# The first norm's modulations computed with the weight tiles as stationary operand

## The reference, cut to what matters

```
mod   = silu(c)     @ w_mod + b_mod      # w_mod is 1024 x 6144
mod_c = silu(c_ctx) @ w_mod + b_mod
sh1, sc1, ... = split(mod, 6);  sh1c, sc1c, ... = split(mod_c, 6)
hc = rmsnorm(ctx, norm1_g) * (1 + sc1c) + sh1c
hx = rmsnorm(x,   norm1_g) * (1 + sc1)  + sh1
proj_x = hx @ w_in                       # then four mixers, gates, FFN, second block
```

## Time and profile before

| | |
|---|---|
| median of 3 runs | 1709.49 us (1703.62 to 1711.7) |
| profiled execution | 1702.95 us |
| its span in the profile | 1701.1 us |
| PE busy | 1641.2 us, 96% of the span |
| PEld busy | 1333.6 us, 78% |
| DVE busy | 909.9 us, 53% |
| ACT busy | 625.5 us, 37% |
| mean granted TensorE clock | 0.984 |

### The profile page before, as it was taken

The page is one execution under the profiler, slowest core; times in us unless marked ns, Lnnn a source line. Parts: engine busy times, 40 slices in busy tenths (PEclk is TensorE's granted clock), DMA queues, the critical chain, the costliest instruction groups (busy, mean ns, idle before and its releaser), DMA issues.

```text
span 1701.1 us, 20100 instructions
## 1 busy us (share of the span) xinstructions
PE 1641.2 (96%) x7909; PEld 1333.6 (78%) x7909; DVE 909.9 (53%) x1248; ACT 625.5 (37%) x805; POOL 92.6 (5%) x130
## 2 busy tenths in 40 slices
PE   8999999899999899999999999999999999999997
PEld 3578778678887688888888889977767788888885
DVE  5774686477666544544344565235776544444323
ACT  2342467422223333333333433245754322222221
POOL 0100000111110000000000100003330000000000
PEclk9999999999999899999999999999999999999998
DMA  9332001544553233332333421223442243332331
GB/s 321 126 119 89 29 25 44 181 163 161 196 173 124 62 105 92 92 97 84 100 87 107 124 75 52 75 64 89 101 126 75 79 113 97 91 93 69 101 102 49
DMA packets 227363, 176.68 MB, mean 104 GB/s; under 512 B 15812, under 2 KB 213316, under 8 KB 227270
## 3 DMA queue, kind: packets, MB, share of 16 engines
q1 hardware_dynamic: 220662, 151.23, 30.5%
q0 software_dynamic: 6608, 24.19, 4.3%
HBM read 166.84 MB, written 2.13 MB: 99 GB/s over the span
## 4 chain that ended last, share of the span: by engine, by line
PE 82%; DVE 10%; ACT 5%; issue 2%; DMA 1%; DVEq 0%; POOL 0%; SPq 0%; POOLq 0%; ACTq 0%
PE PS L452 23%; PE PS L454 23%; PE PS L453 23%; PE PS L2300 2%; DVE T L92 1%; DVE WL L92 1%; PE PS L461 1%; PE PS L586 1%; ACT WH L88 1%; PE PS L976 1%; ACT NTP L88 1%; PE PS L473 1%; PE PS L475 1%; PE PS L474 1%; DMA MSRC<-in_w_mod 1%
## 5 line engine op out<-in xcount | busy, mean ns | idle before, releaser
L452 PE MATMUL PS<-XH,WH 128*128 128x512 f32 (+1 forms) x1280 | 489.6, 382 | 12.5 <-DVE WL L92 10.6
L453 PE MATMUL PS<-XL,WH 128*128 128x512 f32 (+1 forms) x1280 | 484.6, 379 | 0.0
L454 PE MATMUL PS<-XH,WL 128*128 128x512 f32 (+1 forms) x1280 | 484.3, 378 | 0.0
L92 DVE TENSOR_TENSOR WL<-WS,WH 128x2048 fp32r<-128x2048 f32 (+1 forms) x129 | 272.5, 2112 | 214.1 <-ACT WH L88 211.6
L452 PEld LDWEIGHTS PS<-XH,WH 128*128 128x128 f32 x1280 | 239.9, 187 | 61.4 <-DVE WL L92 13.6
L454 PEld LDWEIGHTS PS<-XH,WL 128*128 128x128 f32 x1280 | 239.8, 187 | 45.7
L453 PEld LDWEIGHTS PS<-XL,WH 128*128 128x128 f32 x1280 | 240.0, 188 | 44.4 <-issue 0.7
L88 ACT ACTIVATE WH<-WS 128x2048 fp32r<-128x2048 f32 (+1 forms) x129 | 228.6, 1772 | 71.1 <-PE PS L454 46.7
L452 PE MATMUL PS<-HH,WH 128*128 128x512 f32 x352 | 137.2, 390 | 0.2 <-DVE WL L92 0.2
L453 PE MATMUL PS<-HL,WH 128*128 128x512 f32 x352 | 136.9, 389 | 0.0
L454 PE MATMUL PS<-HH,WL 128*128 128x512 f32 x352 | 136.9, 389 | 0.0
(11 more groups left out here) (359 smaller groups left out, 2245.6 us busy)
## 6 DMA issues: line engine op xcount, KB each, us to landing
WS<-in_w_in SPq DMA_DIRECT2D x24, 1024.0 KB, 5.4
WS<-in_ffn_w_up SPq DMA_DIRECT2D x44, 512.0 KB, 5.0
WS<-in_ffn_w_in SPq DMA_DIRECT2D x44, 512.0 KB, 5.0
MSRC<-in_w_mod POOLq DMA_DIRECT2D x32, 512.0 KB, 4.9
WS<-in_fox_w_in SPq DMA_DIRECT2D x16, 1024.0 KB, 5.6
WS<-in_ffn_w_down SPq DMA_DIRECT2D x16, 704.0 KB, 4.5
WS<-in_ffn_w_out SPq DMA_DIRECT2D x16, 704.0 KB, 4.5
MODW<-in_w_mod SPq DMA_DIRECT2D x8, 1024.0 KB, 10.9
```

The source lines that it names most:

```text
L92: self.e.tensor_tensor(o, a, b, op).then_inc(*self.done.to(*key))
L452: e.matmul(o, lh, rh, start=first and i == 0, stop=False)
L453: e.matmul(o, lh, rl, start=False, stop=False)
L454: ins = e.matmul(o, ll, rh, start=False, stop=last and i == n - 1)
```

## The change

`mod_pe(i)` swaps the two operands. The stationary operand is now a 128x128 piece of the tile, and the two columns of `CA` move through it: 2 halves x 8 rows, 16 instructions a tile instead of 8. The result is already a column for each 128 channels, so `MROW`, `mod_turn_pe`, `mod_rows_dve` and `mod_dve` go. Tiles are paired, i with i + 4: tile p holds shifts and tile p + 4 the scales of the norm's rows 2p and 2p + 1. `mods_dve(p)` adds the bias and makes the scale of these two rows as soon as tile p + 4 is done. The four pairs use banks 7, 5, 0 and 1.

The order changes on every engine. PE: filt1, tile 0, filt2, tile 4, filt3 0 to 2, the sums, tile 1, filt3 3 and 4, the spread, tile 5, filt3 5 to 7, spectrum 0, tile 2, spectrum 1, tiles 6, 3 and 7, spectrum 2 and 3. SP loads `x` right after tile 0, and the tiles in the order 0, 4, 1, 5, 2, 6, 3, 7, with `dft` ahead of the last four. ACT squares three rows before the second sine and copies the spread from the bank to `RST`. DVE multiplies each row of the norm once, by scale and inverse together (`norm1_scaled_dve`); ACT adds the shift in its rounding and DVE in the low half. Spectrum 0 and 1 wait for `mods` 1 and 0, because their banks are shared.

```diff
@@ -181,7 +181,6 @@
-    MROW = zone("MROW", [2, 2048], F32, 36)
     KR = zone("KR", [128, 4, L], F32, 0)
@@ -198,7 +197,7 @@
     MODW = [sbt(f"MODW{i}", [128, 8, 256], F32, o) for i, o in enumerate(
-        (WO[0], WO[1], WO[0] + 8 * U8, WO[1] + 8 * U8, FIX + 16 * U8, FIX, FIX + 8 * U8, XO))]
+        (WO[0], WO[1], WO[0] + 8 * U8, WO[1] + 8 * U8, FIX + 16 * U8, FIX, FIX + 8 * U8, ZO + 24 * U8))]
@@ -577,34 +576,36 @@
+    MPAIR = (7, 5, 0, 1)
...
+        p = i % 4
         e.wait_ge(*landed(f"mod_in{i}"))
...
             e.wait_ge(*acts.at("cact"))
-        for k in range(8):
-            ins = e.matmul(bank(4 + i // 2, 256, p1=2, off=256 * (i % 2)), CA[:, :, k], MODW[i][:, k, :],
-                           start=k == 0, stop=k == 7)
+        if i in (2, 3):
+            e.wait_ge(*dve.at("filt", 7))
+        for m in range(2):
+            for k in range(8):
+                ins = e.matmul(bank(MPAIR[p], 2, off=4 * (i // 4) + 2 * m), MODW[i][:, k, 128 * m:128 * m + 128],
+                               CA[:, :, k], start=k == 0, stop=k == 7)
         ins.then_inc(*pe.to("w", i))
-    def mod_turn_pe(e, b):
-        if b == 0:
-            e.wait_ge(*landed("ident"))
-        e.wait_ge(*dve.at("mod_rows", b))
-        for m in range(4 * b, 4 * b + 4):
-            ins = e.matmul(bank(4, 2, off=256 + 2 * m), MROW[:, 128 * m:128 * m + 128], ID[0:2, 0:2], start=True, stop=True)
-        ins.then_inc(*pe.to("mod_turned", b))
-    def mod_rows_dve(v, b):
-        v.e.wait_ge(*pe.at("w", 2 * b + 1))
-        v.cp(MROW[:, 512 * b:512 * b + 512], bank(4 + b, p1=2), key=("mod_rows", b))
-    def mod_dve(v):
-        v.e.wait_ge(*pe.at("mod_turned", 3))
-        c = VOFF["b_mod"]
-        v.tt(MT[:, 0:16, :], bank(4, 32, off=256).rearrange("p (m j) -> p m j", j=2),
-             VT[:, c:c + 16].unsqueeze(2).broadcast_to([128, 16, 2]), ALU.add, key=("mods",))
+    def mods_dve(v, p):
+        v.e.wait_ge(*pe.at("w", 4 + p))
+        c, g1 = VOFF["b_mod"], VOFF["norm1_g"]
+        v.tt(MODT[:, 0:32].rearrange("p (h q) -> p h q", h=2)[:, :, 4 * p:4 * p + 4].rearrange(
+                 "p h (m j) -> p h m j", j=2),
+             bank(MPAIR[p], 8).rearrange("p (h m j) -> p h m j", h=2, j=2),
+             VT[:, c:c + 16].rearrange("p (h q) -> p h q", h=2)[:, :, 2 * p:2 * p + 2].unsqueeze(3).broadcast_to(
+                 [128, 2, 2, 2]), ALU.add, key=("mods", p))
+        a = SM[:, A1 + 2 * p:A1 + 2 * p + 2]
+        v.ts(a, MT[:, 8 + 2 * p:10 + 2 * p, 0], 1.0, None, ALU.add)
+        v.tt(a, a, VT[:, g1 + 2 * p:g1 + 2 * p + 2], ALU.mult)
@@ -633,12 +634,12 @@
             e.wait_ge(*pool.at("row0"))
-        if i == 2:
-            e.wait_ge(*dve.at("mods"))
+        if i < 2:
+            e.wait_ge(*dve.at("mods", 1 - i))
         if i >= 2:
...
         if i == 3:
-            e.wait_ge(*dve.at("norm1", "rooted", 7))
+            e.wait_ge(*acts.at("norm1", "inverse"))
         for odd in range(2):
@@ -662,29 +663,30 @@
         mod_pe(e, 0)
-        mod_pe(e, 1)
         e.wait_ge(*landed("filt_w2"))
...
         e.matmul(bank(1, p1=64), FW2[:, :], FS1[0:64, :], start=True, stop=True).then_inc(*pe.to("filt2"))
-        mod_pe(e, 2)
-        mod_pe(e, 3)
-        mod_turn_pe(e, 0)
         mod_pe(e, 4)
-        e.wait_ge(*pool.at("ones"))
+        for n in range(3):
+            filt3_pe(e, n)
         e.wait_ge(*dve.at("norm1", "sum", 7))
         sums_pe(e, "norm1", T[2], L, True, True, ("norm1", "sums"), step=1)
+        mod_pe(e, 1)
+        filt3_pe(e, 3)
+        filt3_pe(e, 4)
+        e.wait_ge(*landed("ident"))
+        spread_pe(e, "norm1", L)
         mod_pe(e, 5)
-        mod_turn_pe(e, 1)
-        spread_pe(e, "norm1", L)
+        for n in range(5, 8):
+            filt3_pe(e, n)
+        spectrum_pe(e, 0)
+        mod_pe(e, 2)
+        spectrum_pe(e, 1)
         mod_pe(e, 6)
-        mod_turn_pe(e, 2)
+        mod_pe(e, 3)
         mod_pe(e, 7)
-        filt3_pe(e, 0)
-        mod_turn_pe(e, 3)
-        for n in range(1, 8):
-            filt3_pe(e, n)
-        for i in range(4):
-            spectrum_pe(e, i)
+        spectrum_pe(e, 2)
+        spectrum_pe(e, 3)
@@ -701,9 +703,14 @@
+    def norm1_scaled_dve(v, k):
+        v.stt(SQT[:, k, 0:L], xk(k), SM[:, A1 + k:A1 + k + 1], RST[:, 0:L], ALU.mult, ALU.mult,
+              key=("norm1", "scaled", k))
...
         v.e.wait_ge(*acts.at("norm1", "hi", k))
-        v.tt(XLT[:, k, 0:L], SQT[:, k, 0:L], XHT[:, k, 0:L].bitcast(F32), ALU.subtract, key=("norm1", "lo", k))
+        v.stt(XLT[:, k, 0:L], SQT[:, k, 0:L], modcol(0, k), XHT[:, k, 0:L].bitcast(F32), ALU.add, ALU.subtract,
+              key=("norm1", "lo", k))
@@ -713,31 +720,28 @@
         sine_dve(v, bank(1, p1=64), "f_b2", 2)
-        mod_rows_dve(v, 0)
         for k in range(8):
             square_dve(v, "norm1", k)
-        mod_rows_dve(v, 1)
+        mods_dve(v, 0)
+        e.wait_ge(*landed("decay"))
+        filt_dve(v, 0)
+        filt_dve(v, 1)
+        e.wait_ge(*landed("ident"))
         diagonal_dve(v, "norm1", L)
-        mod_rows_dve(v, 2)
-        e.wait_ge(*pe.at("norm1", "spread"))
+        for n in range(2, 8):
+            filt_dve(v, n)
+        e.wait_ge(*acts.at("norm1", "inverse"))
         for k in range(8):
-            v.tt(SQT[:, k, 0:L], xk(k), bank(3), ALU.mult, key=("norm1", "rooted", k))
-        mod_rows_dve(v, 3)
-        mod_dve(v)
-        g1 = VOFF["norm1_g"]
-        for j, col in ((0, A1), (1, AC)):
-            v.ts(SM[:, col:col + 8], MT[:, 8:16, j], 1.0, None, ALU.add)
-            v.tt(SM[:, col:col + 8], SM[:, col:col + 8], VT[:, g1:g1 + 8], ALU.mult)
-        e.wait_ge(*landed("decay"))
-        for n in range(8):
-            filt_dve(v, n)
-        for k in range(8):
-            v.ts(SQT[:, k, 0:L], SQT[:, k, 0:L], SM[:, A1 + k:A1 + k + 1], modcol(0, k), ALU.mult, ALU.add,
-                 key=("norm1", "scaled", k))
+            if k in (2, 4, 6):
+                mods_dve(v, k // 2)
+            norm1_scaled_dve(v, k)
             if k:
                 norm1_rest_dve(v, k - 1)
+        lo_chunk(v, PROJ)
         norm1_rest_dve(v, 7)
-        lo_chunk(v, PROJ)
+        g1 = VOFF["norm1_g"]
+        v.ts(SM[:, AC:AC + 8], MT[:, 8:16, 1], 1.0, None, ALU.add)
+        v.tt(SM[:, AC:AC + 8], SM[:, AC:AC + 8], VT[:, g1:g1 + 8], ALU.mult)
         for i in range(4):
@@ -763,19 +767,24 @@
         a.act(FS1[0:64, :], FA[:, :], ACT.Sin, key=("sine", 1))
+        e.wait_ge(*landed("x"))
+        for k in range(3):
+            square_act(a, "norm1", k, xk(k))
         e.wait_ge(*dve.at("angle", 2))
         a.act(FS1[0:64, :], FA[:, :], ACT.Sin, key=("sine", 2))
-        e.wait_ge(*landed("x"))
-        for k in range(8):
+        for k in range(3, 8):
             square_act(a, "norm1", k, xk(k))
...
         filt_abs_act(a, 0)
-        hi_chunk(a, PROJ)
+        e.wait_ge(*pe.at("norm1", "spread"))
+        a.act(RST[:, 0:L], bank(3), ACT.Copy, key=("norm1", "inverse"))
         for k in range(8):
-            normed_act(a, "norm1", k, SQT[:, k, 0:L], XHT[:, k, 0:L])
-            if k in (2, 5):
-                spectrum_act(a, k // 3)
+            if k == 6:
+                hi_chunk(a, PROJ)
+            normed_act(a, "norm1", k, SQT[:, k, 0:L], XHT[:, k, 0:L], modcol(0, k))
+            if k in (1, 5):
+                spectrum_act(a, k // 4)
         spectrum_act(a, 2)
@@ -2591,18 +2600,17 @@
         load(FW2[:, :], A["filt_w2"], "filt_w2")
-        for i in range(3):
-            mod_in_load(e, i)
-        load(ID[:, :], A["ident"], "ident")
-        mod_in_load(e, 3)
+        mod_in_load(e, 0)
         load(X[:, :, :], xsrc, "x")
         mod_in_load(e, 4)
-        mod_in_load(e, 5)
         load(FW3[:, :], A["filt_w3"], "filt_w3")
         load(FD[:, :, :], A["decay"].rearrange("(k p) n -> p k n", p=128), "decay")
-        mod_in_load(e, 6)
-        mod_in_load(e, 7)
+        load(ID[:, :], A["ident"], "ident")
+        mod_in_load(e, 1)
+        mod_in_load(e, 5)
         load(FC[:, :, :, :], A["dft"].rearrange("(k p) (x n) -> p k x n", p=128, x=2), "dft")
+        for i in (2, 6, 3, 7):
+            mod_in_load(e, i)
         for j in range(RAW, PROJ + 3):
```

## The result

The changed kernel takes 1735.0 us (median of 6 runs, 1728.17 to 1737.83) against 1706.55 us for the kernel before in the same rounds (1703.24 to 1711.98, 6 runs). The ratio is 1.0157, with a 95% interval of 1.0137 to 1.0177: it is slower by 1.6%. The prediction was 1736 with a range of 1710 to 1753. The profiled execution took 1729.63 us, 26.7 more than the one before.

What follows compares the result with a forecast made beforehand. PE's unbroken row of work in the front was taken as the bound: projections starting at 95.0 instead of 68.4 us add 26.6 to 1702.95, giving 1729.6, and 6.5 more for the median gives 1736 us, range 1710 to 1753.

Steps and rivals of the forecast that it cites:

- A tile at the low clock: PE's front: a new tile's 32 passes at 0.22 us each take 7.04 us, against 3.55 at the high clock.
- The clock is low in busy, narrow tiles: PE's front: low level expected in most tiles and much of the wide passes behind each; the forecast has 60%.
- The rival in which the clock stays up: PE's front: the clock holds, projections start 1.5 us later, time 1711 us; chance 20%.
- The third rival: PE's tiles: weight loads cost 0.111 us at either level, only wide passes suffer; 13.6 us late, 1723 us; chance 10%.
- The stretches: PE's front from 8.0 us, summed piece by piece with the clock's changes: projections start at 95.0 us, 26.6 later.
- my two delays: PE's clock in the front: rises 4.5 us after wide passes begin, falls 3 us after they end.
- the sign that I had named: Profile after: granted clock at 0.50 between 60 and 85 us, where tiles 6, 3 and 7 run.
- The step from there to the median: Whole time: 6.5 us added to the profiled execution's 1729.6, as in the runs before, giving 1736.
- Spectrum 0's hole: PE ahead of spectrum 0: a wait of 3.8 us for `mods` 1 on DVE behind the last filter product.
- At the high clock the order does not pay: PE's front: 4.4 us gained on paper, but holes in the new order start the projections at 69.9, 1.5 us later.
- DVE and ACT: Front: DVE's 6.2 us behind tile 7 hide under spectra 2 and 3 (6.9); ACT's spread copy lies under tile 5.

Runs made afterwards that it cites:

- e1: Changed kernel with the two activation columns sent through each weight piece 64 times (128 columns moving), same loads and order; 1712.09 us, ratio 1.0025.
- e3: Kernel before in its own order, tile operands swapped alone (2 columns moving), turns and row copies gone; 1734.91 us, ratio 1.0162.
- e6: e1 with nine extra 512-column float32 matmuls on constants in PE's waits, result unused; 1707.8 us, ratio 1.0003.
- e9: e1 with POOL's two filter-weight additions waiting for the norm's seventh addition on DVE; 1720.56 us in a single execution.
- e4: Kernel before in its own order, operands swapped with 128 columns moving, no turns; 1700.52 us, ratio 0.9958.

## Why the prediction was right

By its own steps:

- **A tile at the low clock.** Predicted 32 x 0.22 = 7.04 us. Measured 6.8 to 6.9 from start to start (the rows are 6.96 to 6.99 long); 32 loads in tile 0 take 6.90 us, 0.21 to 0.22 apart. At the high clock 3.55 was predicted and 3.5 to 3.6 measured.
- **The clock is low in busy, narrow tiles.** This was the choice that decided, and it came true for the reason given. e1 against the changed kernel shows it: same loads, same order, 1.0025 against 1.0157. The rival in which the clock stays up is out: e3 runs 96 narrow passes in a row, 20.6 us without a gap, at the low level. With it falls, for such passes, the rule of the Trainium skill's page TensorE: Matmul & The Clock Gate, section Why this matters for your kernels, that an engine kept without idle gaps keeps its clock. For wide work e6 agrees with the rule: with the holes filled the clock stays at 1.00 from 26 us on.
- **The third rival** (loads of 0.111 us at either level) is out: they are 0.21 to 0.22 us apart at the low one. There the trace disagrees with the Trainium skill's page TensorE: Matmul & The Clock Gate, section LDWEIGHTS (loading the stationary operand), which gives one rate.
- **The stretches.** Tile 0, filt2 and tile 4 were to end at 24.0 us; they end at 24.6, for tile 4 lands at 17.7. Then my two delays, a rise 4.5 us after wide passes begin and a fall 3 us after they end, missed both ways. I let the clock rise 4.5 us into the first `filt3` passes, but it stayed low through them, the sums and tile 1, and 38.2 stands where I had 34.7. Later it was up more than I priced: spectrum 1 took 3.5 us (5.7), the three tiles 15.4 (18.2), the last two spectra 8.3 (9.1). So 92.65 came out where 95.0 was forecast. Of the sign that I had named, a granted clock of 0.50 between 60 and 85 us, the part from 75 us on came true; from 62 to 74 it was 1.00. The misses cancel in part, and the agreement to 1 us in the median is closer than the method. My forecast for the profiled execution, 1729.6, is as near to its 1729.63 by the same luck: 2.3 us less in the front, 2.3 more in the second block. The step from there to the median was lucky too: I added 6.5 us, from three runs of the kernel before; its six runs lie 3.6 us above its profiled execution, those of the changed kernel 5.4.
- **Spectrum 0's hole.** Predicted 3.8 us behind the last `filt3`, released by `mods` 1; the trace has 3.66 us and names DVE's MODT.
- **At the high clock the order does not pay.** Predicted 1.5 us later than before. With the wide form and the clock held (e6) the projections start at 72.1 us, 3.7 later, 2.2 more than I had. The norm's sums stand at 27.25 us there, where I had 24.9, and nothing behind them is off by more than 0.2 us. I had missed that POOL's additions, moved forward beside DVE's, slow DVE (e9): in e6 two DVE instructions beside them are long by 1.8 us in all. The rest is tile 0, which ends 0.6 us later than I had it. What the order costs in all, its holes and the clock behind them, is seen between e4 and e1, the same form in both: 0.9958 against 1.0025, 65.4 against 76.5 us. With narrow tiles it costs nothing that shows (1.0162 in the old order, 1.0157 in the new).
- **DVE and ACT.** As said, their edits don't show: behind tile 7 (84.3) DVE has the first weight chunk done at 90.7, before the spectra end. A scaled row takes 0.75 us, not the 0.7 I used.

Not tried: the old 256-column form in the new order, and a number of moving columns between 32 and 128.

## What to carry to other kernels

Before swapping operands so that weights are stationary and a few columns move, count what streams. A pass costs its weight load in any case, and in this kernel passes with 2 moving columns, and with 32, ran for the most part at 1.2 GHz, which doubled their cost and that of the wide passes behind them. If the swap is worth it, try more moving columns, even repeated ones: here 128 cost next to nothing more a tile than 2 do at the high clock (3.6 to 3.7 us against 3.5 to 3.6) and, in the order of before, turned +1.6% into -0.4%. And price a hole in TensorE's row at more than its length, for the clock may fall behind it.

## What was not expected of the hardware

- The granted-clock column can show 1.00 at the beginning where the clock is low. In e3 it shows 1.00 from 10 to 70 us, while every narrow pass is at the low level's distance, and e3's mean, 0.984, is that of the kernel before. In the changed kernel it shows 1.00 up to 46 us, though tiles 0, 4 and 1 are low, and 0.50 for the first time from 48 us. Up to the first change that the column shows, only the distance from start to start can be trusted:

```profile
10.00:40.00 30.00, 30.00 (x135) 1.00 1.07 345
40.00:70.00 30.00, 30.00 (x130) 1.00 0.33 108
```

- DVE and POOL hinder each other. In the changed kernel two instructions of the second angle take 1.64 us each instead of 0.68, beside POOL's two additions, which take 3.35 us instead of 2.59; there the second sine is 1.9 us late. e9 shows the same by moving POOL's work.

```profile
18.89 4.04 DVE L103 SCALAR_TENSOR_TENSOR FA<-FK,FA 64x512 f32<-64x512 f32 x3
```

```profile
19.03 3.35 POOL L92 TENSOR_TENSOR FWC<-FW 65x512 f32<-65x512 f32 x2 [17.36 <-DMA FW<-in_filt_w]
```
